# One tile's final RMSNorm scaling, moved from VectorE to ScalarE and GpSimd, with its stores put last

## What is computed

```python
def rmsnorm(x, g):
    xf = x.astype(jnp.float32)
    y = xf * lax.rsqrt(jnp.mean(xf * xf, -1, keepdims=True) + EPS)
    return (y * g.astype(jnp.float32)).astype(x.dtype)

def reference(x, c, ctx, ..., u_emb, v_emb, g_final):
    ...
        x = x + ga2 * peer(modulate(rmsnorm(x, g_ffn[l]), sh2, sc2), w_query[l], sub_keys[l], u_emb[l], v_emb[l])
    ...
    return rmsnorm(x, g_final)
```

## Time and profile before

| | us |
|---|---|
| median of 3 runs | 3571.27 |
| the three runs | 3569.60, 3571.27, 3574.85 |
| the profiled execution, its whole time | 3571.93 |
| its span in the profile | 3569.8 |
| outside the span (3571.93 less 3569.8) | 2.1 |
| last matrix product ends, from the span's start | 3554.0 |
| last scaling on VectorE ends | 3566.6 |
| last store is issued | 3566.7 |

### The profile page before, as it was taken

The page is one execution under the profiler, slowest core; times in us unless marked ns, Lnnn a source line. Parts: engine busy times, 40 slices in busy tenths (PEclk is TensorE's granted clock), DMA queues, the critical chain, the costliest instruction groups (busy, mean ns, idle before and its releaser), DMA issues.

```text
span 3569.8 us, 45979 instructions
## 1 busy us (share of the span) xinstructions
PE 3460.3 (97%) x17471; PEld 2992.0 (84%) x17471; DVE 2146.7 (60%) x3761; ACT 1108.3 (31%) x1245; POOL 1953.7 (55%) x938
## 2 busy tenths in 40 slices
PE   5799999999899999999999999999999999999998
PEld 2578888775688889999999999999888888888886
DVE  1546655114513487993677877673576777767666
ACT  3222211233223223233333443343233323332333
POOL 0344442211444346676566556657777778777764
PEclk8899999999999999999999999999999999999999
DMA  9666642238634226777676677769998889888872
GB/s 347 217 207 189 213 141 77 89 106 309 235 130 154 87 91 224 277 277 273 247 281 266 259 289 280 292 240 347 353 337 325 325 317 330 324 322 314 329 284 98
DMA packets 292279, 874.73 MB, mean 245 GB/s; under 512 B 17913, under 2 KB 78665, under 8 KB 238272
## 3 DMA queue, kind: packets, MB, share of 16 engines
q1 hardware_dynamic: 227024, 519.08, 41.8%
q0 software_dynamic: 38688, 281.15, 19.4%
q10 hardware_dynamic: 26448, 72.98, 5.4%
HBM read 803.78 MB, written 69.32 MB: 245 GB/s over the span
## 4 chain that ended last, share of the span: by engine, by line
PE 87%; DVE 6%; DMA 5%; issue 1%; ACT 1%; ACTq 1%; POOL 0%; DVEq 0%; SPq 0%
PE bank L1915 80%; DMA ring<-in_w_mod 3%; PE bank L2240 2%; DMA neurons<-tiny 2%; PE bank L2123 2%; PE bank L2095 1%; PE bank L1923 1%; DVE low L1341 1%; PE bank L2223 0%; PE bank L2048 0%; DVE hT_lo L1336 0%; DVE acc L1813 0%; ACTq L793 0%; DVE b L1701 0%; PE bank L2187 0%
## 5 line engine op out<-in xcount | busy, mean ns | idle before, releaser
L745 POOL TENSOR_TENSOR split<-ring,split 128x1024 fp32r<-128x1024 f32 x544 | 1305.9, 2413 | 626.3 <-ACT split L1048 624.6
L1915 PE MATMUL bank<-h_hi,split 128*128 128x384 f32 (+1 forms) x4608 | 1225.3, 342 | 4.7 <-POOL split L745 3.6
L1048 ACT ACTIVATE split<-ring 128x1024 fp32r<-128x1024 f32 x544 | 577.2, 1062 | 1558.4 <-PE bank L1915 1534.7
L1915 PE MATMUL bank<-split,a_split 128*128 128x512 f32 x4608 | 1045.0, 389 | 0.1
L1915 PEld LDWEIGHTS bank<-split,a_split 128*128 128x128 f32 x4608 | 864.8, 188 | 180.1 <-POOL split L745 0.5
L1915 PEld LDWEIGHTS bank<-h_hi,split 128*128 128x128 f32 x4608 | 838.6, 188 | 25.4 <-POOL split L745 4.6
L1915 PE MATMUL bank<-h_lo,split 128*128 128x384 f32 (+1 forms) x2304 | 784.8, 341 | 0.0
L1915 PEld LDWEIGHTS bank<-h_lo,split 128*128 128x128 f32 x2304 | 433.4, 188 | 9.5
L447 POOL TENSOR_TENSOR ring_lo<-ring,w_hi 128x2048 fp32r<-128x2048 f32 x47 | 219.6, 4671 | 399.1 <-ACT w_hi L440 399.1
L1804 DVE TENSOR_TENSOR acc<-acc,bank 128x512 f32<-128x512 f32 x372 | 251.5, 683 | 289.7 <-PE bank L1915 282.7
L1915 PE MATMUL bank<-hT_hi,w_hi 128*128 128x512 f32 (+1 forms) x768 | 288.1, 375 | 17.3 <-POOL ring_lo L447 5.3
(11 more groups left out here) (287 smaller groups left out, 3644.4 us busy)
## 6 DMA issues: line engine op xcount, KB each, us to landing
ring<-in_u_emb SPq DMA_DIRECT2D x128, 1024.0 KB
ring<-in_v_emb SPq DMA_DIRECT2D x128, 1024.0 KB
ring<-in_w_mod SPq DMA_DIRECT2D x64, 1024.0 KB
ring<-in_w_in SPq DMA_DIRECT2D x48, 1024.0 KB
ring<-in_w_mod SPq DMA_DIRECT2D x64, 512.0 KB, 4.6
neurons<-tiny ACTq DMA_DIRECT2D x128, 192.0 KB
gate_table<-b ACTq DMA_DIRECT2D x6, 4096.0 KB, 14.6
weigh<-neurons SPq DMA_DIRECT2D x32, 768.0 KB
```

The lines of the kernel that those rows point to most:

```text
L745: nc.gpsimd.tensor_tensor(split[:, r % 2, 1, at].bitcast(F32R), ring[:, r % 4, :, :].rearrange("p k n -> p (k n)")[:, at], split[:, r % 2, ...
L1048: nc.scalar.activation(split[:, q % 2, 0, at].bitcast(F32R), ring[:, q, :, :].rearrange("p k n -> p (k n)")[:, at], ACT.Copy)\
L1915: last = mm(out_, left[a].bitcast(F32R), right[b].bitcast(F32R), start=start and n == 0, stop=stop and n == 2)
```

## The change

`finish(0)` leaves DVE but for its reciprocal. ACT multiplies tile 0 in place with 1/rms (a Copy activation with a per-partition scale), in two halves of 1024 columns, between the square root of tile 0 and the squaring of tile 1's last quarter. It first waits for the reciprocal (`y_step` 3). After each half it raises `tile_scaled`, and POOL multiplies that half in place with the row `g_final_row` and raises `first_made`. DVE goes from tile 0's reciprocal straight to `merge(127, 2)`, then `finish(1)` and `finish(2)` as before. SP issues the stores in the order tile 1, tile 2, tile 0; those of tile 0 wait for `first_made`. Nothing else is changed.

```diff
@@ sync
-            for j in range(JD):
+            for j in (1, 2, 0):
                 for h in range(2):
                     at = slice(h * 1024, (h + 1) * 1024)
-                    sp.wait_ge(y_made, 2 * j + h + 2)
+                    if j:
+                        sp.wait_ge(y_made, 2 * (j - 1) + h + 2)
+                    else:
+                        sp.wait_ge(first_made, h + 1)
                     sp.dma_start(out[0, j * P:(j + 1) * P, at], acc[:, j, at]).then_inc(out_stored, 16)
@@ gpsimd, at the end
+            for h in range(2):
+                at = slice(h * 1024, (h + 1) * 1024)
+                pool.wait_ge(tile_scaled, h + 1)
+                nc.gpsimd.tensor_tensor(acc[:, 0, at], acc[:, 0, at], g_final_row[:, at], op=ALU.mult)\
+                    .then_inc(first_made, 1)
@@ scalar, in the loop over o
                     nc.scalar.activation(rms3[:, j:j + 1], hssq[:, 4 * j + 3:4 * j + 4], ACT.Sqrt,
                                          bias=ssq3[:, j:j + 1], scale=1.0 / D).then_inc(x_rms, 1)
+                if o == 9:
+
+                    act.wait_ge(y_step, 3)
+                    for h in range(2):
+                        at = slice(h * 1024, (h + 1) * 1024)
+                        nc.scalar.activation(acc[:, 0, at], acc[:, 0, at], ACT.Copy, scale=rstd3[:, 0:1])\
+                            .then_inc(tile_scaled, 1)
@@ vector
                 if unit == NK - 1:
-                    finish(0)
+                    dve.wait_ge(x_rms, 8)
+                    nc.vector.reciprocal(rstd3[:, 0:1], rms3[:, 0:1]).then_inc(y_step, 1)
```

More of the change, by code:

```diff
@@ L425, in hybrid_layer @@
         y_squared = sem("y_squared")
+        tile_scaled = sem("tile_scaled")
+        first_made = sem("first_made")
         y_made = sem("y_made")
```

## The result

The changed kernel took 3576.78 us at the median of 16 runs (3570.32 to 3580.74), the kernel before 3570.86 us (16 runs, 3567.41 to 3576.37). The ratio is 1.0017, with a 95% interval of 1.001 to 1.0024: slower by about 0.17%, inside the 0.2% that the prediction called no change that can be told (the upper end of the interval lies beyond it), and on the side to which it leaned. The predicted time was 3575.6 us.

A forecast was written before the change was run, and what follows sets the result against it. TensorE bounds until 3554.0, then VectorE, with store transfers close behind. VectorE and GpSimd taking turns, then six queued stores (7.8 us) and 0.9 us, end the span at 3574.1, +4.3: 3571.27 + 4.3 = 3575.6 us, range 3571.0 to 3579.0.

The forecast's parts named there:

- The bound: TensorE's last product ends at 3554.04; the change touches only the 15.8 us after it, 0.44% of the span.
- the held addition: VectorE's addition in merge(127, 2) waits for GpSimd's first piece, taking 2.7 us in place of 0.69.
- the layout: Changed end, VectorE and GpSimd taking turns: VectorE ends 1.7 us later than before, not 2.4 earlier.
- The step that the trace had left open: Tile 1's first scaling on VectorE is held by GpSimd's second piece, about 3.3 us in place of 1.28.
- The sum: Span's end moves from 3569.8 to 3574.1, +4.3 us, six stores following one another after late VectorE.
- the case in which nothing is held: Rival: GpSimd holds no VectorE instruction, finish(1) waits only for ScalarE; +1.3 us, 3572.6 us, chance 0.07.
- Only the merge held: Rival: GpSimd holds the merge's addition but not tile 1's scaling; +2.3 us, 3573.5 us, chance 0.11.
- GpSimd's multiplication in place being slow: Rival: GpSimd's pieces take 4.0 us each, held twice against VectorE; +7.8 us, 3579.1 us, chance 0.06.
- The stores don't bound: Rival: six final stores move faster than one after another, so VectorE's end counts; 3570.0 us, chance 0.04.

The follow-up runs named there:

- e5: Kernel before with every dense quarter's gate and residual moved early and late banks gated in PSUM; 11.03 us from last product to span's end, ratio 1.0024.
- e7: Early-gate kernel with tile 0 on ScalarE and GpSimd, norm's row in PSUM, stores as halves become ready; 11.09 us after last product, ratio 1.0018.
- e3: Changed kernel without GpSimd's two multiplications, tile 0's stores waiting for ScalarE; 17.14 us from last product to span's end, ratio to kernel before 1.0003.
- e2: Changed kernel with the stores' order put back to tile 0, 1, 2; 17.42 us from last product to span's end, ratio to kernel before 1.0005.
- e4: Changed kernel with the norm's row copied to PSUM for VectorE's scalings of tiles 1 and 2; 17.92 us after last product, ratio to before 1.0002.
- e8: Changed kernel unaltered, run once more; 19.88 us from last product to span's end, median 3574.86 us, ratio to kernel before 1.0009.
- e1: Kernel before with only the stores' order changed to tile 1, 2, 0; 18.31 us from last product to span's end, ratio 1.0005.
- e9: Kernel before with the early gate and residual for the last column quarter alone; 14.09 us from last product to span's end, ratio 0.9998.
- e10: Kernel before with the early gate and residual for the last two column quarters; 12.28 us after last product, median 3568.25 us, ratio 0.9991.
- e6: Early-gate kernel with VectorE's finish of tile 0 ahead of tile 1's last merge; 10.91 us from last product to span's end, ratio 1.002.

## Why the prediction was right

**The bound.** That nothing before 3554 would move, and that the last 15.8 us are all there is to win or lose, held for this change: 3554.04 and 3554.11. (It isn't so for every edit of the end: e5 to e7, which reach into the units before, made the last product some 12 us later.)

**ScalarE.** The new activations were put at 1.06 us each, by the rounding of the same size, which has no scale; they took 1.133 and 1.148. Tile 1's root came at 3559.89 + 0.29 = 3560.18, where 3560.1 was said. As reckoned, this delay was hidden behind the held addition in the changed kernel; e3 shows it bare, 1.22 us.

**GpSimd against VectorE.** The addition was said to end at 3561.15 and ended at 3561.12; the second piece 3563.41 and 3563.31; the first scaling 3564.55 and 3564.39; VectorE's end 3568.35 and 3568.18. There was some luck in it: the layout needs GpSimd's first piece to come before the addition, with 0.3 us to spare by the forecast, and it had 0.09 (3558.22 against 3558.31; 0.08 or 0.09 in e2, e4 and e8 too). No run shows the other order. The step that the trace had left open, whether a scaling is held, was settled as the forecast took it: 3.17 us beside GpSimd, and with the row in PSUM 2.47 for a pair, 1.28 each (e4). The rule cited from the Trainium skill, page "SBUF — State Buffer", section "Who interferes with whom", is that a VectorE instruction with two inputs in SBUF contends with a GpSimd instruction that reads SBUF, and that the first one has the shared port for its whole length. All of these rows agree with it.

**The stores.** First issue 3564.6 said, 3564.42 measured; six transfers in 7.8 us, both; 0.9 us behind them, both. The sum was +4.3 us and is 4.1 in the spans. One aside was wrong: the +1.3 us of the case in which nothing is held was also called the cost of the order by itself. That price (1.4 in e3) is the order's less what VectorE gains when the scaling leaves it; by itself, with the scaling on VectorE, the order costs 2.5 us (e1). Neither the sum nor a chance rested on it.

**The rivals.** Only the merge held: +2.3 was its price, and e4, which makes it true, has 17.92 - 15.76 = 2.2. Nothing held: +1.3, and e3 has 1.4. GpSimd's multiplication in place being slow: its pieces took 2.34 and 2.19 of their own. The stores don't bound: the changed kernel's transfers have no gap, and e1, with VectorE as before, ended 2.5 us later by their order alone. (The price of this rival, 3570.0, also took nothing to be held.)

**The median.** The forecast was 4.3 us above before; the medians say 5.9 and, the second time, 3.5. The first interval, 1.001 to 1.0024, is 3.6 to 8.6 us and takes in the forecast; what of the 5.9 is more than scatter stays open, since the ends in the two profiles show 4.0 and 4.1.

**Where an expectation failed** is in the experiments, not in the prediction: e5 named TensorE's waiting as its rival and put no price on it. The rows of e5 show the price: held instructions of 2.7 us in front of the flushes, 7.9 us of waiting, and 4.4 us more at half clock and in taking up work again. In e9 and e10 VectorE was less far ahead than expected, by 0.5 and 0.9 us.

## What to carry to other kernels

Before work moves from VectorE to GpSimd, count the inputs in SBUF on both: here every instruction of VectorE with two of them took turns with GpSimd's (2.81 us in place of 0.69, 3.17 in place of 1.28), so the work moved came back as waiting, and one operand kept in PSUM let the two run side by side. Look at the last transfers as a queue of its own: pieces that are ready early should be issued early, since at the end the stores' own time, here 7.8 us, can be the bound. And where an engine's lateness is to be cured by moving its work forward, the idle time there has to be free of whoever waits for that engine: the same idea lost 0.2% with 24 instructions moved and won some 0.1% with 12, by an interval that just reaches 1.

## What the runs showed of the hardware

Three things had not been expected. ScalarE's 128x1024 Copy in place with a per-partition scale took 1.13 to 1.15 us, where the rounding Copy into another tile, without a scale, took 1.06; which of the differences costs it no run shows. VectorE's multiplication of a PSUM bank in place by a row in SBUF (128x512) took 0.70 us at most, about as long as one with both inputs in SBUF (0.69), also beside GpSimd's pieces (e7).

The third is TensorE's clock. After it had waited 3.6 and 2.9 us for banks, its granted clock stayed at 1.00 for the first 0.4 to 1 us of work, fell to 0.50, and was back at 1.00 some 4 us after the work began again; each time cost about 1.7 us. After waits of 0.35, 0.84 (e10) and 1.05 us it stayed at 1.00. e5, e6 and e7 are alike in this; in e6, where the first long wait ended 3.3 us earlier, the low stretch is earlier by about as much (a window of e6, columns as in e5):

```profile
3501.50:3504.80 3.30, 3.30 (x9) 2.56 (x8) 3.23 (x6) 0.00 (x0) 0.00 (x0) 0.50 0.49 191
```

So a wait that another engine's lateness puts on TensorE can cost more than its own length.
